# Mixture-of-experts stage: 32 passes of one expert with two column halves in place of 47 passes of 128 slots

## What is computed

```
grp = argmax(x @ w_rg + b_rg)
top_val, top_idx = top_k((x @ w_re[grp]) + b_re, 2)
gate = softmax(top_val) * p_grp
y_e = (silu(x @ w_gate[e]) * (x @ w_up[e])) @ w_down[e]
out = layer_norm(alpha * x + sum over the two experts of gate * y_e)
```

## Time and profile before

| | |
|---|---|
| median of 3 runs | 3565.77 us (3563.08 to 3568.21) |
| span of the profiled execution | 3561.8 us |
| TensorE busy (matmul) | 3398.4 us, 95% |
| VectorE, ScalarE, GpSimd busy | 1575.2, 900.8, 262.2 us |
| DMA | 370.56 MB |
| expert stage, first transpose to first final gather | 2960.1 to 3503.9 us of the span |

### The profile page before, as it was taken

The page is one execution under the profiler, slowest core; times in us unless marked ns, Lnnn a source line. Parts: engine busy times, 40 slices in busy tenths (PEclk is TensorE's granted clock), DMA queues, the critical chain, the costliest instruction groups (busy, mean ns, idle before and its releaser), DMA issues.

```text
span 3561.8 us, 30860 instructions
## 1 busy us (share of the span) xinstructions
PE 3398.4 (95%) x12332; PEld 1852.5 (52%) x12332; DVE 1575.2 (44%) x2801; ACT 900.8 (25%) x1752; POOL 262.2 (7%) x251
## 2 busy tenths in 40 slices
PE   9999999899999999999999999999999988999997
PEld 3458546666654444444444565774557434444443
DVE  6345477566631655554635212324666142211114
ACT  4110363377751100000000112213334031111112
POOL 1013232000000000000000000000000002222221
PEclk9999999999999999999999999999999998999999
DMA  6114213000022111110210101002000109999994
GB/s 233 36 66 150 115 50 112 16 1 1 1 95 95 59 37 46 47 46 26 96 47 33 63 24 38 24 10 100 1 24 1 49 40 381 368 364 370 369 361 165
DMA packets 63243, 370.56 MB, mean 104 GB/s; under 512 B 6827, under 2 KB 13243, under 8 KB 37501
## 3 DMA queue, kind: packets, MB, share of 16 engines
q1 hardware_dynamic: 40492, 187.71, 14.5%
q0 software_dynamic: 22608, 180.89, 13.5%
HBM read 329.16 MB, written 39.41 MB: 103 GB/s over the span
## 4 chain that ended last, share of the span: by engine, by line
PE 86%; ACT 6%; DVE 6%; DMA 1%; issue 1%; SPq 0%; POOL 0%; DVEq 0%; ACTq 0%; POOLq 0%
PE ps L1305 14%; PE ps L2638 9%; PE ps L1432 7%; PE ps L1607 6%; PE ps L837 5%; PE ps L2657 5%; PE ps L2236 3%; PE ps L1609 3%; PE ps L1236 3%; PE ps L984 2%; PE ps L703 2%; PE ps L840 2%; PE ps L1012 2%; PE ps L646 2%; ACT arena L1063 2%; PE ps L2076 2%
## 5 line engine op out<-in xcount | busy, mean ns | idle before, releaser
L1305 PE MATMUL ps<-arena 128*128 128x512 f32 x1232 | 529.9, 592 | 1.1 <-DVE arena L1336 1.1
L1305 PEld LDWEIGHTS ps<-arena 128*128 128x128 f32 x1232 | 233.5, 190 | 297.3 <-issue 286.9
L2638 PE MATMUL ps<-arena 128*128 128x512 f32 x752 | 331.1, 593 | 0.0
L1432 PE MATMUL ps<-arena 128*128 128x512 f32 x616 | 264.6, 592 | 0.0
L2596 POOL DMA_INDIRECT arena<-in_wgu_dram,arena x47 | 44.2, 940 | 2610.8 <-DVE arena L2556 2359.0
L2638 PEld LDWEIGHTS ps<-arena 128*128 128x128 f32 x752 | 139.3, 190 | 157.9 <-issue 157.9
L1607 PE MATMUL ps<-arena 128*128 128x512 f32 x480 | 209.6, 597 | 0.0
L1432 PEld LDWEIGHTS ps<-arena 128*128 128x128 f32 x616 | 116.6, 189 | 147.9 <-issue 143.8
L1118 DVE TENSOR_SCALAR_CACHE_REDUCE arena<-ps 128x1280 f32<-128x1280 f32 x96 | 139.3, 1488 | 111.8 <-PE ps L984 111.8
L837 PE MATMUL ps<-arena 128*128 128x512 f32 (+1 forms) x432 | 172.8, 553 | 0.0
L2657 PE MATMUL ps<-arena 128*128 128x512 f32 x376 | 169.2, 592 | 0.5 <-DVE arena L2708 0.5
(11 more groups left out here) (381 smaller groups left out, 4931.7 us busy)
## 6 DMA issues: line engine op xcount, KB each, us to landing
arena<-in_wmod_dram SPq DMA_DIRECT2D x24, 1024.0 KB, 5.0
yslot<-arena SPq DMA_DIRECT2D x47, 512.0 KB
arena<-in_wup_dram SPq DMA_DIRECT2D x22, 1024.0 KB, 4.8
arena<-in_wout_dram SPq DMA_DIRECT2D x16, 1024.0 KB, 4.9
arena<-in_cf_dram SPq DMA_DIRECT2D x12, 1024.0 KB, 4.8
arena<-in_wdn_dram SPq DMA_DIRECT2D x16, 704.0 KB, 4.1
arena<-in_w2b_dram SPq DMA_DIRECT2D x9, 1024.0 KB, 4.8
arena<-in_ci_dram SPq DMA_DIRECT2D x16, 512.0 KB, 3.5
```

The source lines that it names most:

```text
L1305: ins = mm(bk(b), left[:, k], right[:, k], k == 0, k == 3)
L1432: ins = mm(bk(b), sb(left + k * 128, 128), right(k), k == 0, k == 10)
L2638: ins = mm(bk(b), sb(XB + i % 2 * 1024 + k * 128, 128), sb(WGU[i % 3] + k * 512, 512), k == 0, k == 7)
```

## The change

A pass now belongs to one expert, so NBLK = 32. Its 128 slots are two halves of 64. The left half holds the expert's first 64 rows. The right half holds its second 64 rows; if the expert has no more than 64, the half is free, and is given to a guest: a block of 64 rows of an expert that has more than 128. Each `mm` of gate, up and down becomes two, each with 64 stationary columns, its own weights, and its own half of the partitions of the bank.

The left weights are loaded by SyncE with plain DMAs (`sp_own_gu`, `sp_own_dn`), three buffers each, the first ones already during the stage before (`sp_tokens`). The right weights are made in two steps: VectorE copies the whole gate and up buffer (`dve_guest_gu`), ScalarE the down buffer (`act_guest_dn`), and then GpSimd gathers over the copy (`pool_guest_gu`, `pool_guest_dn`) with indices that lie beyond the bound of 4095 where the half has no guest, for which the gather is told to leave the rows out. TensorE waits for the own load and for this gather. `dve_place` works out blocks of 64, guests and hosts, and computes `slots` ahead of `widx`; the final gathers' indices come last. The diagonals of the final sum are now made in passes 31 and 32 (counted from 0, of 34), and the loads of the last layer norm's gains come in pass 31. Nothing is changed outside of this.

```diff
-NBLK = 47
+NBLK = 32
...
+    def sp_token_rows(j):
+        S.wait_ge(*(yield ("xk", j, 1)))
+        LD.ready()
+        dma.dma_start(out=x_d[j * 128:(j + 1) * 128, :], in_=sb(XK + j * 1024, 1024)).then_inc(*LD.turn(("xd", j)))
+
     def sp_tokens():
-        for j in range(8):
-            S.wait_ge(*(yield ("xk", j, 1)))
-            LD.ready()
-            dma.dma_start(out=x_d[j * 128:(j + 1) * 128, :], in_=sb(XK + j * 1024, 1024)).then_inc(*LD.turn(("xd", j)))
+        S.wait_ge(*(yield ("mval", NM - 1)))
+        for i in range(3):
+            sp_own_dn(i)
+        for j in range(2):
+            yield from sp_token_rows(j)
+        S.wait_ge(*(yield ("w", nth["wout2"][6])))
+        sp_own_gu(0)
+        S.wait_ge(*(yield ("w2o", 1, 7)))
+        sp_own_gu(2)
+        for j in range(2, 4):
+            yield from sp_token_rows(j)
+        S.wait_ge(*(yield ("logit", 1)))
+        sp_own_gu(1)
+        for j in range(4, 8):
+            yield from sp_token_rows(j)
...
+        vt.tensor_scalar(nb, bk(b, 32, off=256), 1 / 64, 31.5 / 64, MUL, ADD).then_inc(*V.step())
...
+            vt.tensor_tensor(slot_t[:, half16], slot_e[:, half16], con("tok").rearrange("p (j u) -> p j u", u=1).broadcast_to([128, 8, 32]),
+                             MUL).then_inc(*V.step())
+            vt.tensor_tensor(slot_a[:, half16], wide("iota", 128), pm[:, half16].rearrange("p (j u) -> p j u", u=1).broadcast_to([128, 8, 128]),
+                             ALU.is_equal).then_inc(*V.step(("slotoh", q)))
...
+        V.wait_ge(*(yield ("owners",)))
+        vt.tensor_scalar(be, bk(bank["owners"], NBLK), con("pidx"), None, ADD).then_inc(*V.step())
+        vdone()
+        vt.tensor_copy(widx.bitcast(U32), be).then_inc(*V.step(("widx",)))
...
-    WGU = [M_WR, M_WR + 4096, WB]
-    WDN = [WB + 10240, WB + 4096, WB + 6144, WB + 8192]
-    DIAG = WB + 12288
+    OWN_GU = [M_WR + 4096, M_WR, B2 + 4096]
+    OWN_DN = [LG - 6144 + 2048 * i for i in range(3)]
+    GUEST_GU = [B2 + 8192, B2 + 12288]
+    GUEST_DN = [B2, B2 + 2048]
+    assert GUEST_GU[1] + 4096 <= OWN_DN[0]
+    DIAG = OWN_GU[(NBLK - 3) % 3]
     LG2 = DIAG + 2048
-    FS = LG2 + 2048
     GYS = [BIG + 2048 * q for q in range(4)] + [M_WR + 2048 * q for q in range(4)]
+    gusem = [nc.alloc_semaphore(f"own_gate_up{i}") for i in range(3)]
+    dnsem = [nc.alloc_semaphore(f"own_down{i}") for i in range(3)]
 
     def by_row(idx):
         return bass.IndirectOffsetOnAxis(ap=idx, axis=0)
 
-    def pool_weights(i):
-        to = by_row(widx.bitcast(U32)[:, i:i + 1])
-        if i > 2:
-            G.wait_ge(*(yield ("egu", i - 3)))
+    def sp_own_gu(i):
+        dma.dma_start(out=sb(OWN_GU[i % 3], 4096), in_=X["wgu"][128 * i:128 * i + 128, :]).then_inc(gusem[i % 3], 16)
+
+    def sp_own_dn(i):
+        dma.dma_start(out=sb(OWN_DN[i % 3], 2048), in_=X["wed"][128 * i:128 * i + 128, :]).then_inc(dnsem[i % 3], 16)
+
+    def gu_ready(i):
+        return gusem[i % 3], 16 * (i // 3 + 1)
+
+    def dn_ready(i):
+        return dnsem[i % 3], 16 * (i // 3 + 1)
+
+    def pool_guest_gu(i):
+        G.wait_ge(*(yield ("cg", i)))
         GD.ready()
-        gt.indirect_dma_start(sb(WGU[i % 3], 4096), None, X["wgu"], to).then_inc(*GD.turn(("wgu", i)))
-        if i > 3:
-            G.wait_ge(*(yield ("edn", i - 4)))
+        gt.indirect_dma_start(sb(GUEST_GU[i % 2], 4096), None, X["wgu"], by_row(widx.bitcast(U32)[:, i:i + 1]),
+                              bounds_check=4095, oob_is_err=False).then_inc(*GD.turn(("bg", i)))
+
+    def pool_guest_dn(i):
+        G.wait_ge(*(yield ("cd", i)))
         GD.ready()
-        gt.indirect_dma_start(sb(WDN[i % 4], 2048), None, X["wed"], to).then_inc(*GD.turn(("wed", i)))
+        gt.indirect_dma_start(sb(GUEST_DN[i % 2], 2048), None, X["wed"], by_row(widx.bitcast(U32)[:, i:i + 1]),
+                              bounds_check=4095, oob_is_err=False).then_inc(*GD.turn(("bd", i)))
...
     def pool_experts():
-        G.wait_ge(*(yield ("widx",)))
         G.wait_ge(*(yield ("xk", 7, 1)))
-        yield from pool_weights(0)
         G.wait_ge(*(yield ("slots",)))
         for j in range(8):
             G.wait_ge(*(yield ("xd", j)))
         yield from pool_rows(0)
         yield from pool_rows(1)
-        yield from pool_weights(1)
-        for i in range(2, NBLK):
-            yield from pool_rows(i)
-            yield from pool_weights(i)
+        G.wait_ge(*(yield ("widx",)))
+        for i in range(NBLK + 1):
+            if i + 2 < NBLK:
+                yield from pool_rows(i + 2)
+            if i < NBLK:
+                yield from pool_guest_gu(i)
+            if i:
+                yield from pool_guest_dn(i - 1)
...
-        P.wait_ge(*(yield ("wgu", i)))
+        P.wait_ge(*gu_ready(i))
+        P.wait_ge(*(yield ("bg", i)))
         for k in range(8):
-            ins = mm(bk(b), sb(XB + i % 2 * 1024 + k * 128, 128), sb(WGU[i % 3] + k * 512, 512), k == 0, k == 7)
+            for side, w in enumerate((OWN_GU[i % 3], GUEST_GU[i % 2])):
+                rows = 64 * side, 64 * side + 64
+                ins = mm(bk(b, 512, *rows), sb(XB + i % 2 * 1024 + k * 128 + 64 * side, 64), sb(w + k * 512, 512), k == 0, k == 7)
...
-        P.wait_ge(*(yield ("wed", i)))
+        P.wait_ge(*dn_ready(i))
+        P.wait_ge(*(yield ("bd", i)))
         for h2 in range(2):
             yield from claim(6 + h2)
             for k in range(2):
-                ins = mm(bk(6 + h2), sb(HB + 512 + i % 2 * 256 + k * 128, 128), sb(WDN[i % 4] + k * 1024 + h2 * 512, 512), k == 0, k == 1)
+                for side, w in enumerate((OWN_DN[i % 3], GUEST_DN[i % 2])):
+                    rows = 64 * side, 64 * side + 64
+                    ins = mm(bk(6 + h2, 512, *rows), sb(HB + 512 + i % 2 * 256 + k * 128 + 64 * side, 64),
+                             sb(w + k * 1024 + h2 * 512, 512), k == 0, k == 1)
...
+    def act_guest_dn(i):
+        A.wait_ge(*dn_ready(i))
+        if i > 1:
+            A.wait_ge(*(yield ("edn", i - 2)))
+        else:
+            A.wait_ge(*(yield ("didx",)))
+            A.wait_ge(*(yield ("slotsum",)))
+        st.activation(sb(GUEST_DN[i % 2], 2048), sb(OWN_DN[i % 3], 2048), ACT.Copy).then_inc(*A.step(("cd", i)))
...
+                yield from act_guest_dn(i - 1)
                 A.wait_ge(*(yield ("egu", i - 1)))
...
+    def dve_guest_gu(i):
+        V.wait_ge(*gu_ready(i))
+        if i > 1:
+            V.wait_ge(*(yield ("egu", i - 2)))
+        vt.tensor_copy(sb(GUEST_GU[i % 2], 4096), sb(OWN_GU[i % 3], 4096)).then_inc(*V.step(("cg", i)))
...
-                vt.tensor_scalar(xk, xk, ALPHA, None, MUL).then_inc(*V.step())
-                for q, gf in enumerate((g1f, g2f)):
-                    vt.tensor_scalar(sb(DIAG + (2 * (i - 4) + q) * 128, 128), ident, gf[:, i - 4:i - 3], None, MUL).then_inc(*V.step(("diag", i - 4)))
+                vt.tensor_scalar(xk, xk, ALPHA, None, MUL).then_inc(*V.step(("xscaled", i - 4)))
...
+            if i < NBLK:
+                yield from dve_guest_gu(i)
+            if i >= NBLK - 1 and i < NBLK + 1:
+                V.wait_ge(*(yield ("egu", NBLK - 3)))
+                for j in range(4 * (i - NBLK + 1), 4 * (i - NBLK + 1) + 4):
+                    for q, gf in enumerate((g1f, g2f)):
+                        vt.tensor_scalar(sb(DIAG + (2 * j + q) * 128, 128), ident, gf[:, j:j + 1], None, MUL).then_inc(*V.step(("diag", j)))
...
-        for i in range(NBLK):
-            S.wait_ge(*(yield ("eyc", i, 0)))
-            S.wait_ge(*(yield ("eyc", i, 1)))
-            LD.ready()
-            dma.dma_start(out=ys_d[i * 128:(i + 1) * 128, :], in_=sb(YB + i % 2 * 1024, 1024)).then_inc(*LD.turn(("ys", i)))
+        for i in range(1, NBLK + 2):
+            if 3 <= i + 2 < NBLK:
+                S.wait_ge(*(yield ("egu", i - 1)))
+                sp_own_gu(i + 2)
+            if i == NBLK - 1:
+                yield from sp_gains()
+            if 3 <= i + 1 < NBLK:
+                S.wait_ge(*(yield ("edn", i - 2)))
+                sp_own_dn(i + 1)
+            if i >= 2:
+                S.wait_ge(*(yield ("eyc", i - 2, 0)))
+                S.wait_ge(*(yield ("eyc", i - 2, 1)))
+                LD.ready()
+                dma.dma_start(out=ys_d[(i - 2) * 128:(i - 1) * 128, :], in_=sb(YB + i % 2 * 1024, 1024)).then_inc(*LD.turn(("ys", i - 2)))
```

147 lines of the change are left out of this document (88 added, 59 removed).

## The result

The changed kernel takes 3418.15 us, median of 4 runs (3410.84 to 3424.78), against 3565.11 us for the kernel before in the same runs: a ratio of 0.9588 (95% interval 0.9573 to 0.9603). The forecast was 3406 us within 3396 to 3452. The profiled execution took 3420.63 us, with a span of 3419.3 us at a mean granted clock of 0.982; the span before was 3561.8.

The account below looks back on a forecast made before the run. The prediction took TensorE to bound the kernel, DMA at most 1.6 us per pass behind. Span 3561.8 - 170.9 + 6.4 + 5 = 3402.3 us, with 4.0 kept from span to median: 3406 us, range 3396 to 3452.

Parts of the forecast that it names:

- Passes gone, -170.9: Expert stage: 47 passes become 32, so fifteen passes of 11.39 us go, -170.9 us.
- Halves side by side: Expert matmuls: the two 64-column halves of a pair run at the same time, ratio 1.00 to 1.01 from line 1010.
- the third rival of the list: Expert matmuls: halves don't run side by side at 512 columns, 10.3 us per pass more, 3736 us; chance 0.04.
- The form, +0.2 per pass, +6.4: Expert matmuls: splitting products by columns costs 0.2 us per pass, +6.4 us (0 to +31), changes of form included.
- Copies, 0: Expert passes: VectorE's copy of 2.7 us and ScalarE's of 2.1 us are covered and cost nothing.
- Entry, +5 (+2 to +9): Placement to first gate and up: slots +2, row gather -1.3, uncovered first copy and gather +4; together +5 us.
- VectorE's copy beside GpSimd: Skill's rule: copy holds the row gather, pushing guests' issue from 5.3 to 6.3; covered passes unchanged, entry +1 us, 3407.
- The new wait, 0: Gate, up and down wait for own weights and bounded gathers; 7.2 us of cover for gate and up, costed at nothing.
- the second rival: Expert passes: chain copy, gather, matmul becomes the bound, 4.1 us per pass, +131, 3537 us; chance of late gather 0.13.
- A skipped row is moved all the same: First rival, guests' gathers: 3.15 MB more per pass, DMA becomes the bound, 3585 to 3668 us; chance 0.09.
- From span to time, +4.0: Whole kernel: median of the runs lies 4.0 us above the profiled span, kept to turn 3402.3 into 3406 us.
- End, 0: After the last passes: diagonal scalings move to the last two passes, final gathers wait as today; 0 us.

Follow-up runs that it names:

- the run with undivided products: Changed kernel with undivided 128-column products using own weights for both halves, gathers, copies and waits kept: 3426.65 us, ratio 0.9621.
- The experiment with four changes: Kernel with guests' gathers ahead of the row gather, first bank of down left undivided, giving four changes of form per pass: 3420.17 us, passes 12.04 us.
- the exchanged copies: Changed kernel with ScalarE copying gate and up and VectorE copying down, instead of the reverse: 3407.47 us in one run.
- with the rows behind the guests: Changed kernel with GpSimd issuing both bounded guests' gathers ahead of the gather of rows two passes on: 3409.66 us, ratio 0.9567.

## Why the prediction was right, and where it was not

*Passes gone, -170.9*: right, -171.0. In the run with undivided products a pass is 11.39 us, so the new loads, copies and gathers cost TensorE nothing in a covered pass.

*Halves side by side*: right; the third rival of the list, that they don't run so at 512 columns, is out. *The form, +0.2 per pass, +6.4*: inside 0 to +31, but a pass measured 0.30 more, +8.8 over the 30 passes behind the entry, and the step that failed is "the two changes of form per pass, transposes to products and back, I take as inside this, since line 1010's block has both edges in its 2.34 us". The experiment with four changes puts 0.15 us on each. Line 1010's block doesn't deny it, and that its ratio of 1.00 to 1.01 came so near to a pair's true price was luck. Read start by start in the trace of before, it has the same edges: its first pair takes 0.05 us more than the others (which take 0.109), its last 0.10 more, and the instruction of line 1022 behind it, outside the 2.34 us, 0.26 us where it is 0.20 after line 1012. The block of line 1012 that I held beside it was no clean measure: its first instruction takes 0.213 us and the others 0.112, so it loses as much as the edges cost. The estimate that stood beside it, from the Trainium skill, "TensorEngine Tiling (Array Packing)", Key Properties (changing the tiling mode drains the engine), was 0.16 us per change and +10 us; the runs agree with its size, and I had let line 1010 overrule it. That the engine drains at a change is the Trainium skill's word; the runs show only what a change costs.

*Copies, 0*: right. VectorE's took 2.28 us (2.7 expected) and then idled 4.82 us before the product; ScalarE's 1.91 (2.1).

*Entry, +5 (+2 to +9)*: it was +8.7, near the upper end. Slots came 1.5 us later (+2 expected), the transposes 1.3 us later (+0.7), and from there to gate and up it took 2970.63 - 2961.43 = 9.20 us instead of 3.79: +5.4 for the uncovered copy and gather (+4). Three terms were mis-sized. The row gather was to be 1.3 us quicker than before and was 0.2 us quicker (from slots to transposes 5.96 us for 6.16). "Issue 0.94" was 2.69 us beside VectorE's second copy. And the slow matmuls stood only in the upper end: the first gate and up lasted 9.31 us instead of 7.37, +2.0 to the second one. The signal, 1.3 us behind the issue, lay within "1 to 3".

*VectorE's copy beside GpSimd*: the row gather's issue lasted 2.73 us beside the copy and 0.95 us away from it. The Trainium skill, "SBUF — State Buffer", section "SBUF: two separate sides", says that such a copy shuts GpSimd out of the port that it writes descriptors through; the exchanged copies agree, 1.66 us beside a copy of 1.22. What I had this do in a covered pass, push the end of the guests' issue from t = 5.3 to 6.3, it didn't do. The copy ended at 3.97 (4.4 expected), the issue began at 4.77 and ended at 5.76; and with the rows behind the guests, where nothing is held, it begins at 4.77 as well. In a covered pass the hold costs nothing, at the entry 1.7 us by the guests' issue alone (2.69 against 0.99).

*The new wait, 0*: right for the usual landing, 6.4 us. I had set it against 7.2 us of cover, counted from the end of the issue, while the landings are counted from its start; so counted the cover is 8.17 us. The late landings were missed: "I cost both at nothing" used the one landing of the earlier trace rows and no spread; at 11.3 us two passes stalled, +11.1 us with the slow matmuls behind them. This is the mild form of the second rival, in 2 passes of 32 instead of in all.

*A skipped row is moved all the same*: false in bytes, 25.21 MB in the software queue as forecast (25), but half true in packets: each stays one. Its price per pass was sound (17.2 us, its lower end). Its turning point, from 4 to 24% of the guests' bytes on, was worked out as if they were spread evenly over the passes. They come by whole guests, and each makes its own pass late while the passes between stay covered: 8 real guests in 32, a quarter of the bytes, cost 58 us and still give 0.9757. The gain of 147 us would be gone only after 20 to 29 guests, an estimate from 7.3 to 5.1 us each.

*From span to time, +4.0*: I had taken the distance of the median of the runs from the profiled span. Here the profiled execution was one of the slower ones, and the same distance is 3418.15 - 3419.3 = -1.15. *End, 0*: right, -0.1.

So the span came out 17.0 us above the 3402.3 of the sum: forms 2.4, entry 3.7, stalls 11.1, and -0.2 for the rest. The median came out only 12 us above the forecast, because the 4.0 was 5.2 too high: that part is luck. Executions also differ by several us before the stage is reached (slots ready between 2952 and 2960), which is why single spans can't be compared to better than that.

## What to carry to other kernels

When work is dropped by an index out of bounds, count its signal as a full small transfer: it takes its place in the queue, and now and then it lands late, so it goes first in its queue and as early as its buffer allows. Where the cover is 8 us and the usual landing 6, judge by the longest of many landings, not by the median or a single row, and ask how many landings a median rests on. Alternating between undivided and divided products costs per change, so changes are to be counted, not columns; and an edge is read from single starts against its like, not from the sum of a block.
